# New order of work at the joints between the sites of a two-block float32 model

## Chip, core and metric

The kernel runs on one core of one Trainium2 chip. Its time is the device time of one execution in microseconds (us). Before the change three runs gave 1433.32, 1435.70 and 1436.69 us; the median is 1435.7.

## What is computed

256 tokens of width 1024 go through two blocks, all in float32. The first block has two layers (latent attention, convolution, Fourier and gating branches) and ends with a root-mean-square norm. The second block has six sites, in this order: feed-forward, mixer, feed-forward, feed-forward, mixer, feed-forward.

```python
def second_block(x, ...):
    for layer in range(2):
        g = norm_gains[layer]
        h = rmsnorm(x, g[0])
        x = x + 0.5 * rmsnorm(swiglu(h, w_gate[layer, 0], w_up[layer, 0], w_down[layer, 0]), g[1])
        h = rmsnorm(x, g[2])
        x = x + rmsnorm(token_mixer(h, ...), g[3])
        h = rmsnorm(x, g[4])
        x = x + 0.5 * rmsnorm(swiglu(h, w_gate[layer, 1], w_up[layer, 1], w_down[layer, 1]), g[5])
    return x
```

`swiglu(h)` is `(silu(h @ w_gate) * (h @ w_up)) @ w_down` with 2816 hidden features. Between the last sum of one site and the first product of the next lie two norms over all 1024 features: that of the site's result and that of the new `x`.

## The kernel before

**Layout.** `x` (the tile `residual`) holds two token tiles t = 0, 1 of 128 tokens, each in two half rows hf = 0, 1 of 512 features. Products take each number as a high and a low part (`HH`, `HL` for the input, `WH`, `WL` for weights), so one product is three matmuls: high by high, low by high, high by low. Weights come by DMA in slots of 1 MB through a ring of three (`weight_ring`). A slot holds two units of 128 x 1024. Of each unit ScalarE makes the high part (`high(U)`, L992) and VectorE the low part (`low(U)`, L1573). SyncE fills a ring slot again when the low part of the last unit of its old content is counted in `s_low`; `turn` gives each unit its place in that count. `WH` and `WL` hold six units.

**A site's start.** TensorE turns `x` into feature-major chunks c = 0..7 of 128 features (`site_norm`, transposes at L2447, with a few products of constants at L2438 between them). ScalarE copies each chunk with the norm's gain as `HH` (L1032), VectorE takes the rest as `HL` (L1608). The first two units (`first_units`) run chunk by chunk over the high parts (L2474, L2475), then over the low parts (L2479). The norm's own factor is not needed for these products: squares of `x` are summed on ScalarE (`x_square`, L996), VectorE and ScalarE make the inverse root (`inverse`), and TensorE spreads it over the partitions (`norm_sum`, L2464); ScalarE copies it to `norm_row` (L1041). What is read from the products afterwards is multiplied by `norm_row`.

**Feed-forward site.** Each pair of hidden chunks takes six units: gate, up, one earlier down unit, gate, up, down. At the end the last three down units a+4, a+5, a+6 are added into banks 4 to 7, which hold the result y(t, hf). The unit a+4 goes over both tiles; then each of y(0,0), y(0,1), y(1,0), y(1,1) gets a+5 and a+6 in turn.

**Mixer site.** Its products of queries, keys and values take 24 units. The first scores (L2608) need the first query block and its key block, which VectorE reads out by L1756 (`evicted`). VectorE's order there is: units 0 and 1 read out, `low` of units 4 and 5, unit 2 read out. The scores need units 0 and 2.

**A site's end.** ScalarE sums the squares of each y(t, hf) in that order (`site_tail`, L1051) and takes the root per tile (L1057). VectorE multiplies y by the gain (`gained`, L1634), takes the reciprocal (L1639) and adds each half row to `x` (`update`, L1644). Per tile it is: gained 0, gained 1, reciprocal, update 0, update 1. At the end of a feed-forward site ScalarE first makes the high parts of three units of the next site (`ahead`), then loads the table for the square root (L1120), then starts on the squares.

**Block joint.** The last product of the first block is scaled by VectorE (L1278). GpSimd adds three of the four half rows to `x` (L671) and VectorE one (L1282). ScalarE sums squares (L1008), VectorE scales `x` (`final_scaled`, L1582), tile by tile, with `low` of units 0, 2 and 1 of the first site between these steps. The first site starts with the units 0 and 1, one gate and one up.

Each engine works through its instructions in the order in which they are written; waits are on semaphores.

## Time and profile before

| | |
|---|---|
| median of three runs | 1435.7 us |
| the profiled execution | 1436.06 us |
| its span, first to last instruction | 1434.1 us |
| TensorE (PE) busy | 1398.1 us, 97% |
| VectorE (DVE) busy | 1018.7 us, 71% |
| ScalarE (ACT) busy | 726.7 us, 51% |
| GpSimd (POOL) busy | 86.7 us, 6% |
| DMA | 243.03 MB, mean 169 GB/s |
| mean granted TensorE clock | 0.997 of full speed |

TensorE is busy for nearly all of the span, but that includes the products of constants at the joints. The time between the last useful product of one site and the first of the next is what an order of work at a joint can change. Matmul durations overlap: of a row that holds several, the time to the start of the next row tells more than its length.

### The profile page before, as it was taken

How to read it: one execution, taken by the hardware profiler on the slowest of the kernel's cores; microseconds unless marked ns; L12 is line 12 of the kernel's file. 1: busy time of each engine (PE TensorE's matmuls, PEld its weight loads, DVE VectorE, ACT ScalarE, POOL GpSimd, SP SyncE). 2: the span in 40 equal slices, each digit the busy share in tenths (PEclk: the TensorE clock that was granted, in tenths of full speed). 3: DMA queues.
4: the chain of work that ended last, by engine and by line, in shares of the span. 5: the costliest groups of instructions: out<-in, count | busy, mean ns of one | idle time of the engine just before them, and what ended most of it. 6: DMA issues, size and time to landing. Idle time of an engine off the chain costs nothing.

```text
span 1434.1 us, 22170 instructions
## 1 busy us (share of the span) xinstructions
PE 1398.1 (97%) x8053; PEld 1159.8 (81%) x8053; DVE 1018.7 (71%) x1693; ACT 726.7 (51%) x1244; POOL 86.7 (6%) x103
## 2 busy tenths in 40 slices
PE   5999999999999999999999999999999999999998
PEld 2778747869768888888888888888888888888887
DVE  2588454469677777787686777877777876877776
ACT  3433264345565444475664444654445756644444
POOL 0301211220110000000200000000000002000000
PEclk9999999999999999999999999999999999999999
DMA  9622184275235655754345556646655643455662
GB/s 354 195 88 89 59 285 175 88 221 150 88 133 170 198 189 175 248 176 146 118 133 176 175 193 193 211 153 202 197 183 177 195 142 118 133 176 178 202 196 98
DMA packets 185654, 243.03 MB, mean 169 GB/s; under 512 B 4560, under 2 KB 154608, under 8 KB 185456
## 3 DMA queue, kind: packets, MB, share of 16 engines
q1 hardware_dynamic: 182272, 229.43, 49.9%
q0 software_dynamic: 2736, 10.55, 2.2%
q10 hardware_dynamic: 576, 2.10, 0.4%
q8 instruction: 46, 0.75, 0.2%
q14 instruction: 24, 0.20, 0.0%
HBM read 241.01 MB, written 1.05 MB: 169 GB/s over the span
## 4 chain that ended last, share of the span: by engine, by line
PE 69%; DVE 12%; DMA 9%; ACT 5%; issue 4%; POOL 0%; SPq 0%; DVEq 0%; ACTq 0%; POOLq 0%
PE bank L1977 33%; PE bank L2496 13%; PE bank L2498 7%; DMA weight_ring<-in_w_ffn_up 5%; DVE weights_low L1573 3%; ACT weights_high L992 3%; DVE arena L1567 2%; PE bank L2104 2%; DMA weight_ring<-in_w_ada 2%; DMA weight_ring<-in_w_ffn_down 2%; PE bank L1958 1%; DMA weight_ring<-in_w_in 1%; PE bank L2324 1%; PE bank L2474 1%; PE bank L2475 1%
## 5 line engine op out<-in xcount | busy, mean ns | idle before, releaser
L1573 DVE TENSOR_TENSOR weights_low<-weight_ring,weights_high 128x1024 fp32r<-128x1024 f32 x328 | 393.3, 1223 | 128.8 <-ACT weights_high L992 128.7
L992 ACT ACTIVATE weights_high<-weight_ring 128x1024 fp32r<-128x1024 f32 x328 | 334.6, 1048 | 102.1 <-PE bank L1977 62.0
L2496 PE MATMUL bank<-input_split,weights_high 128*128 128x512 f32 x1280 | 319.5, 391 | 0.0
L2496 PEld LDWEIGHTS bank<-input_split,weights_high 128*128 128x128 f32 x1280 | 234.7, 188 | 45.0
L2498 PEld LDWEIGHTS bank<-input_split,weights_low 128*128 128x128 f32 x1280 | 174.6, 190 | 12.5
L2498 PE MATMUL bank<-input_split,weights_low 128*128 128x256 f32 x1280 | 178.5, 282 | 0.0
L1977 PE MATMUL bank<-weights_high,hidden_high 128*128 128x512 f32 x352 | 138.8, 394 | 1.2 <-DVE hidden_low L1682 1.2
L1066 ACT ACTIVATE silu_gate<-gate_sum 128x256 f32<-128x256 f32 x88 | 36.7, 418 | 202.0 <-DVE gate_sum L1660 200.5
L1977 PE MATMUL bank<-weights_low,hidden_high 128*128 128x512 f32 x352 | 137.9, 392 | 0.0
L1977 PE MATMUL bank<-weights_high,hidden_low 128*128 128x512 f32 x352 | 137.0, 389 | 0.0
L1977 PE MATMUL bank<-input_split,weights_high 128*128 128x256 f32 x576 | 105.6, 285 | 0.0
L1072 ACT ACTIVATE hidden_high<-hidden 128x256 fp32r<-128x256 f32 x88 | 36.8, 418 | 129.8 <-DVE hidden L1673 123.7
L1977 PE MATMUL bank<-weights_high,input_split 128*128 128x256 f32 (+1 forms) x384 | 90.2, 323 | 0.5 <-issue 0.5
L1977 PEld LDWEIGHTS bank<-input_split,weights_high 128*128 128x128 f32 x576 | 89.5, 192 | 1.1 <-DVE qk_feature_major L1756 0.7
L1977 PE MATMUL bank<-hT_high,first_high 128*128 128x512 f32 (+1 forms) x248 | 89.6, 361 | 0.2 <-DVE weight_ring_low L1253 0.2
L1977 PE MATMUL bank<-hT_high,weight_ring_low 128*128 128x512 f32 (+1 forms) x248 | 86.9, 350 | 0.0
L1977 PE MATMUL bank<-input_split,weights_low 128*128 128x256 f32 x288 | 81.4, 283 | 0.0
L1977 PEld LDWEIGHTS bank<-weights_high,hidden_high 128*128 128x128 f32 x352 | 66.4, 189 | 14.3 <-issue 2.8
L1977 PEld LDWEIGHTS bank<-weights_high,hidden_low 128*128 128x128 f32 x352 | 66.1, 188 | 14.5
L1977 PEld LDWEIGHTS bank<-weights_low,hidden_high 128*128 128x128 f32 x352 | 66.4, 189 | 10.7
L1977 PEld LDWEIGHTS bank<-weights_high,input_split 128*128 128x128 f32 x384 | 64.4, 190 | 8.6 <-issue 3.5
L1682 DVE TENSOR_TENSOR hidden_low<-hidden,hidden_high 128x256 fp32r<-128x256 f32 x88 | 37.4, 425 | 43.7 <-ACT hidden_high L1072 43.7
(358 smaller groups left out, 2267.5 us busy)
## 6 DMA issues: line engine op xcount, KB each, us to landing
weight_ring<-in_w_ffn_gate SPq DMA_DIRECT2D x44, 1024.0 KB, 5.3
weight_ring<-in_w_ffn_up SPq DMA_DIRECT2D x44, 1024.0 KB, 5.3
weight_ring<-in_w_ffn_down SPq DMA_DIRECT2D x44, 1024.0 KB, 4.9
weight_ring<-in_w_in SPq DMA_DIRECT2D x32, 1024.0 KB, 5.3
weight_ring<-in_w_ada SPq DMA_DIRECT2D x24, 1024.0 KB, 6.0
weight_ring<-in_w_out SPq DMA_DIRECT2D x16, 1024.0 KB, 5.0
weight_ring<-in_w_in SPq DMA_DIRECT2D x24, 512.0 KB, 4.8
gain_row<-in_norm_gains POOLq DMA_DIRECT2D x6, 512.0 KB, 4.1
```

The lines of the kernel that those rows point to most:

```text
L992: A(unit_in(WH, U), unit_source(U), ACT.Copy).then_inc(s_high, 1)
L1066: A(sgate[:, par, :], gsum[:, par, :], ACT.Silu).then_inc(s_silu, 1)
L1072: A(HBH[:, par if to is None else to, :], hbuf[:, par, :], ACT.Copy).then_inc(s_hh, 1)
L1567: STT(accv, src, w, accv, ALU.mult, ALU.add).then_inc(*done("conv_tap", L, j, k))
L1573: TTn(unit_in(WL, U), unit_source(U), unit_in(WH, U).bitcast(F32), ALU.subtract).then_inc(s_low, 1)
L1682: TTn(HBL[:, to, :], hbuf[:, par, :], HBH[:, to, :].bitcast(F32), ALU.subtract).then_inc(s_hl, 1)
L1958: last = mm(b[32 * k:32 * k + 32, :], CS[:, 4 * q + k, :], quarters(n)[:, k, :], start=(q == 0), stop=(q == 1), skip_group_check=True)
L1977: last = mm(o, lhs(x), rhs(y), start=start and m == 0, stop=stop and m == 2, skip_group_check=True)
L2104: last = mm(b[out_rows, 0:ncol], lhs(k), hT[:, k, 0:ncol], start=(k == 0), stop=(k == KD - 1))
L2324: mm(b[:, 0:keys], Q[0:QK, h, seg * T + qt * P:seg * T + (qt + 1) * P], K[0:QK, h, k0:k0 + keys], start=True, stop=True).then_inc(*done("s ...
L2496: mm(b[:, :].rearrange("p (h n) -> p h n", h=2), unit_in(WH, U)[:, k, :], HX[:, k, :, :], start=(k == 0), stop=False, skip_group_check=True)
L2498: last = mm(b[:, 0:T], unit_in(WL, U)[:, k, :], HH[:, k, :], start=False, stop=(k == KD - 1), skip_group_check=True)
```

## The change

It rearranges the work at all six joints, and adds one instruction on GpSimd and two on VectorE per feed-forward end.

1. Block joint: the first site starts with units 0 and 2 (both gate units of the first slot). VectorE adds three of the four half rows itself; `final_scaled` is cut into five parts, of which (1, 0) comes in two quarters; the high parts of units 1 and 3 and their low parts come later, unit 3's after the load of the Silu table.
2. `x` is turned in two portions: chunks 0 to 3 of both tiles first, and chunks 4 to 7 after the products of chunk 2 (`rest_turned`). The second product of constants is half as wide.
3. At a site's end the half row (1, 0) is added in two quarters before (1, 1) is multiplied by the gain. After a feed-forward site the sum of squares of x(0, 1) moves from ScalarE to VectorE (`tensor_tensor_reduce` over 512 columns).
4. Feed-forward end: a+4 and a+5 are added to y(0,0) and y(0,1) together, then a+6; then each of y(1,0), y(1,1) gets all three. VectorE makes the low parts of a+5 and a+6 before the steps that they stood behind. ScalarE makes the high part of only two units of the next site before the squares; those of the third and fourth follow the roots of tile 0 and tile 1. The low part of the third is made by GpSimd, and VectorE counts it in `s_low` after the last `HL`.
5. Site start: the norm's spreading product comes two chunks later in a feed-forward site and one whole unit later in a mixer; `high` and `low` of the next units and the read-out of the up unit change places.

Renamed semaphores (`q_copied`) and arguments that only pass `rest_turned` on are left out here.

```diff
-X_BANK = (4, 5, 2, 3, 6, 7, 6, 7)
+X_BANK = ((4, 5, 1, 3, 6, 7, 6, 7),) + ((4, 5, 2, 3, 6, 7, 6, 7),) * 5
...
-ADDED = [{(0, 1), (1, 1)}, {(1, 1)}]
+ADDED = [{(0, 1), (1, 1)}, {(0, 1), (1, 0), (1, 1)}]
...
+                if i < 5 and kind == "ffn":
+                    third = unit_base[i + 1] + EARLY - 2
+                    pool.wait_ge(s_high, turn[third] + 1)
+                    pool.tensor_tensor(unit_in(WL, third), unit_source(third), unit_in(WH, third).bitcast(F32), ALU.subtract).then_inc(*done("third_low", i + 1))
...
-                    act.wait_ge(s_used, step(U - SPLIT + 1, j, 6))
+                    act.wait_ge(s_used, step(U - SPLIT + 1 + (U == SPLIT + 1), j, 6))
...
```

ScalarE:

```diff
-                        if t == 1:
-                            x_square(0, 0, 0)
-                            x_square(0, 0, 1)
                 act.wait_ge(*at("final_squares", t, 1))
                 A(stat[:, 8 + t:9 + t], stat[:, 2 * t + 1:2 * t + 2], ACT.Sqrt, bias=stat[:, 28 + t:29 + t], scale=1.0 / D).then_inc(*done("final_root", t))
-                if t == 0:
-                    high(1)
-            high(3)
+            high(1)
...
-                if i:
+                after_ffn = i and SITES[i - 1][0] == "ffn"
+                if i and not after_ffn:
                     x_square(i, 0, 0)
-                    x_square(i, 0, 1)
-                if i and SITES[i - 1][0] == "ffn":
-                    high(unit_base[i] + EARLY - 1)
                 for c in range(KD):
+                    if c == 4:
+                        x_square(i, 1 if i else 0, 0)
...
-                for hf in range(2):
-                    x_square(i, 1, hf)
+                    A(HH[:, c, :], B[X_BANK[i][c]][:, half * T:(half + 1) * T], ACT.Copy, scale=vT[:, 2, R_PRE + 8 * i + c:R_PRE + 8 * i + c + 1]).then_inc(*done("input_high", i, c))
+                if not after_ffn:
+                    x_square(i, 0, 1)
+                if i == 0:
+                    x_square(i, 1, 0)
+                x_square(i, 1, 1)
                 act.wait_ge(*at("x_mean", "ready", i))
                 A(stat[:, 8:10], stat[:, 6:8], ACT.Sqrt).then_inc(*done("rms_ready", "site", i))
-                high(unit_base[i] + 4)
                 if SITES[i][0] == "ffn":
                     A(stat[:, 60:61], eps[:, 0:1], ACT.Silu)
+                if i == 0:
+                    high(3)
+                if SITES[i][0] == "mix":
+                    high(unit_base[i] + 4)
                 act.wait_ge(*at("norm_sum", i))
                 A(norm_row, B[4][:, 0:T], ACT.Copy).then_inc(*done("norm_row", i))
-                high(unit_base[i] + 5)
+                if SITES[i][0] == "mix":
+                    high(unit_base[i] + 5)
 
             def site_tail(i):
                 for t in range(2):
...
+                            if t and i < 5 and SITES[i][0] == "ffn":
+                                x_square(i + 1, 0, 0)
...
+                    if i < 5 and SITES[i][0] == "ffn":
+                        high(unit_base[i + 1] + EARLY - 2 + t)
...
+                high(a + 4)
                 silu(0, f0 + 1, f0 if n else None)
-                if n:
-                    high(a + 6)
-                    hidden_high(0, f0 + 1, None)
-                else:
-                    hidden_high(0, f0 + 1, None)
-                    high(a + 6)
+                hidden_high(0, f0 + 1, None)
+                high(a + 5)
+                high(a + 6)
...
+                high(a + 6)
                 hidden_high(1, f + 2, None, to=2)
-                high(a + 6)
-                for U in ahead[1:]:
+                for U in ahead[1:2]:
...
```

VectorE, the block joint, the site's start and end:

```diff
+                    low(0)
+                    out_scaled(1, 0, 0)
+                    low(2)
+                    out_scaled(1, 0, 1)
+                    out_scaled(1, 1, 0)
+                    out_scaled(1, 1, 1)
+                    return
...
+            final_inverse(0)
+            final_scaled(0, slice(0, 512), 0)
+            final_inverse(1)
+            final_scaled(1, slice(0, 256), 0, "first")
+            final_scaled(1, slice(256, 512), 0)
+            final_scaled(0, slice(512, 1024), 1)
+            final_scaled(1, slice(512, 1024), 1)
...
+                if i and SITES[i - 1][0] == "ffn":
+                    dve.wait_ge(*at("third_low", i))
+                    CP(stat[:, 61:62], eps[:, 0:1]).then_inc(s_low, 1)
+                if i and SITES[i - 1][0] == "ffn":
                     low(unit_base[i] + EARLY - 1)
+                if i == 0:
+                    low(1)
...
+                        if (t, hf) == (0, 1) and i and SITES[i - 1][0] == "ffn":
+                            dve.wait_ge(*at("x_mean", "first tile", i))
...
+                gained(0, 0)
+                gained(0, 1)
+                scale(0)
+                update(0, 0, slice(0, 512))
+                update(0, 1, slice(512, 1024))
+                gained(1, 0)
+                if i == 5:
+                    gained(1, 1)
+                    scale(1)
+                    update(1, 0, slice(0, 512))
+                else:
+                    if SITES[i][0] == "ffn":
+                        dve.wait_ge(*at("x_new", i, 0, 1))
+                        dve.tensor_tensor_reduce(out=XN2[:, 0, 512:1024], in0=X[:, 0, 512:1024], in1=X[:, 0, 512:1024], scale=1.0, scalar=0.0, op0=ALU.mult, op1=ALU.add, accum_out=stat[:, 1:2]).then_inc(*done("x_mean", "first tile", i + 1))
+                    scale(1)
+                    update(1, 0, slice(0, 256), "first")
+                    update(1, 0, slice(256, 512))
+                    gained(1, 1)
+                update(1, 1, slice(512, 1024))
...
+                if n == 0:
+                    low(3)
                 gate_parts(0, a + 1)
-                up_parts(0, a + 2)
-                low(a + 4)
                 dve.wait_ge(*at("norm_row", i))
                 gate_scaled(0, f0 + 1)
+                up_parts(0, a + 2 if n else 3)
+                multiplied(0, f0 + 1)
+                low(a + 4)
+                hidden_low(0, f0 + 1)
                 low(a + 5)
-                multiplied(0, f0 + 1)
-                hidden_low(0, f0 + 1)
...
+                low(a + 5)
                 dve.wait_ge(s_used, a + 4)
                 dve.wait_ge(s_silu, f + 2)
                 TTn(hbuf[:, 1, :], B[3][:, 0:T], sgate[:, 1, :], ALU.mult).then_inc(s_h, 1)
-                low(a + 5)
+                low(a + 6)
                 hidden_low(1, f + 2, to=2)
-                low(a + 6)
-                for U in ahead[1:]:
+                for U in ahead[1:2]:
...
```

TensorE:

```diff
+                        part = (1, 0, "first") if t and c < 2 else (t, c // 4)
+                        pe.wait_ge(*(at("x_new", i - 1, *part) if i else at("final_scaled", *part)))
+                        last = tr(B[X_BANK[i][c]][:, half * T + t * P:half * T + (t + 1) * P], X[:, t, c * P:(c + 1) * P], ident)
...
-                warm(1)
-                turned(0, (4, 5, 6, 7))
-                turned(1, (0, 1, 2, 3, 4, 6, 5, 7))
+                warm(1, 256)
+                turned(1, (0, 1, 2, 3))
+                return lambda: (turned(0, (4, 6)), turned(1, (4, 6)), turned(0, (5, 7)), turned(1, (5, 7)))
...
+                step_to = 1 if i else 2
                 for q in range(2):
-                    pe.wait_ge(s_low, turn[U + q] + 1)
+                    pe.wait_ge(s_low, turn[U + step_to * q] + 1)
                 for c in range(KD):
...
+                    if c == 2:
+                        rest_turned()
...
-                    if site is not None and k == 3:
+                    if site is not None and k == 5:
...
+                second = 1 if n else 2
+                for r in hand_over(0) + hand_over(second):
...
+                first_units(i, a, (B[0], B[second]), T, rest_turned)
+                for r in hand_over(3 - second) + hand_over(3):
                     pe.wait_ge(*at(*r))
-                gate_up(1, a + 2, f0 if n else None, None, i)
+                if n:
+                    gate_up(1, a + 2, f0, None, i)
+                else:
+                    for U, b, site in ((1, 1, i), (3, 3, None)):
+                        pe.wait_ge(s_low, turn[U] + 1)
+                        wide_product(B[b], U, site).then_inc(s_used, 1)
...
+                lasts = ((1, a + 4, f), (0, a + 5, f + 1), (2, a + 6, f + 2))
+                for rest in (lasts[:2], lasts[2:]):
                     for hf in range(2):
-                        for par in range(2):
-                            pe.wait_ge(s_hl, f + 1 + par)
-                            pe.wait_ge(s_low, turn[a + 5 + par] + 1)
-                            last = down_row(2 * par, a + 5 + par, t, False, par == 1, (hf,))
-                            if t and hf:
-                                last.then_inc(s_used, 1)
-
-            def mix(i, n):
+                        for par, U, ready in rest:
+                            pe.wait_ge(s_hl, ready)
+                            pe.wait_ge(s_low, turn[U] + 1)
+                            down_row(par, U, 0, False, U == a + 6, (hf,))
+                for hf in range(2):
+                    for par, U, ready in lasts:
+                        last = down_row(par, U, 1, False, U == a + 6, (hf,))
+                        if hf:
+                            last.then_inc(s_used, 1)
...
+                products(2, 3)
                 norm_sum(i)
-                products(2, 4)
+                products(3, 4)
                 scores(0)
...
```

## Rows read from the trace of the kernel before

**Rows 1.** The page, groups of instructions: busy us, mean ns, idle before and releaser

```profile
L1573 DVE TENSOR_TENSOR weights_low<-weight_ring,weights_high 128x1024 fp32r<-128x1024 f32 x328 | 393.3, 1223 | 128.8 <-ACT weights_high L992 128.7
L992 ACT ACTIVATE weights_high<-weight_ring 128x1024 fp32r<-128x1024 f32 x328 | 334.6, 1048 | 102.1 <-PE bank L1977 62.0
```

**Rows 2.** Waits of TensorE: line, releaser: us in total, times, longest us

```profile
PE bank L2447 <- DVE residual L1644: 2.1, 4, 1.4
```

**Rows 3.** Timeline of TensorE, feed-forward to feed-forward: start us, us, instruction [idle before]

```profile
927.30 1.02 PE L2438 MATMUL bank<-const_base 128*128 128x512 f32 x2
...
930.27 1.32 PE L2447 MATMUL bank<-const_base,residual 128*128 128x128 f32 x8 [0.21 <-DVE residual L1644]
931.34 0.36 PE L2474 MATMUL bank<-input_split,weights_high 128*128 128x256 f32 x1
...
937.18 0.87 PE L2496 MATMUL bank<-input_split,weights_high 128*128 128x512 f32 x3
```

**Rows 4.** Timelines of ScalarE and of VectorE at the same joint

```profile
927.50 0.60 ACT L1051 ACTIVATE silu_gate<-bank 128x512 f32<-128x512 f32 x1 [0.28 <-PE bank L1977]
...
928.22 0.29 ACT L1057 ACTIVATE stat<-stat 128x1 f32<-128x1 f32 x1
...
930.63 2.30 ACT L1032 ACTIVATE input_split<-bank,vectors_T 128x256 fp32r<-128x256 f32 x6
...
929.46 1.41 DVE L1644 SCALAR_TENSOR_TENSOR residual<-x_scaled,stat,residual 128x512 f32<-128x512 f32 x2
931.14 2.45 DVE L1608 SCALAR_TENSOR_TENSOR input_split<-bank,vectors_T,input_split 128x256 fp32r<-128x256 f32 x6 [0.27 <-ACT input_split L1032]
```

**Rows 5.** Timelines of GpSimd and VectorE where both are at work

```profile
275.46 1.29 POOL L671 TENSOR_TENSOR residual_ctx<-residual_ctx,scaled_out 128x512 f32<-128x512 f32 x1 [2.27 <-DVE scaled_out L1278]
...
274.03 0.75 DVE L1221 TENSOR_SCALAR gated<-residual,stat 128x1024 f32<-128x1024 f32 x1
...
275.49 1.82 DVE L1221 TENSOR_SCALAR gated<-residual,stat 128x1024 f32<-128x1024 f32 x1
...
418.69 2.04 DVE L1582 SCALAR_TENSOR_TENSOR residual<-residual,stat,gain_row 128x512 f32<-128x512 f32 x2
```

**Rows 6.** Timelines of TensorE and VectorE, second feed-forward to mixer

```profile
1115.22 1.02 PE L2438 MATMUL bank<-const_base 128*128 128x512 f32 x2
...
1125.18 0.68 PE L2464 MATMUL bank<-scaled_out,const_base 128*128 128x128 f32 x4
...
1131.55 0.49 PE L2608 MATMUL bank<-qk_feature_major 64*128 64x128 f32 x4
...
1129.26 0.42 DVE L1756 SCALAR_TENSOR_TENSOR qk_feature_major<-bank,scaled_out 128x256 f32<-128x256 f32 x1
```

**Rows 7.** Timeline of TensorE, first feed-forward to mixer

```profile
611.28 1.02 PE L2438 MATMUL bank<-const_base 128*128 128x512 f32 x2
...
630.09 0.49 PE L2608 MATMUL bank<-qk_feature_major 64*128 64x128 f32 x4
```

**Rows 8.** Timeline of TensorE, mixer to feed-forward

```profile
739.17 1.02 PE L2438 MATMUL bank<-const_base 128*128 128x512 f32 x2
...
748.60 0.86 PE L2496 MATMUL bank<-input_split,weights_high 128*128 128x512 f32 x3
```

**Rows 9.** Timelines of TensorE and ScalarE, block joint to the first down unit

```profile
424.26 1.82 PE L2447 MATMUL bank<-const_base,residual 128*128 128x128 f32 x8 [2.07 <-DVE residual L1582]
425.74 0.56 PE L2474 MATMUL bank<-input_split,weights_high 128*128 128x256 f32 x1
...
432.50 0.86 PE L2496 MATMUL bank<-input_split,weights_high 128*128 128x512 f32 x3
...
438.55 0.40 PE L1977 MATMUL bank<-weights_high,hidden_high 128*128 128x512 f32 x1
...
431.61 1.28 ACT L1039 ACT_TABLE_LOAD   x1
```

**Rows 10.** A stretch of the block joint: us, busy of each engine, PEclk, DMA share, GB/s

```profile
425.70:428.00 2.30, 2.30 (x13) 2.30 (x12) 1.88 (x5) 1.67 (x6) 0.04 (x1) 0.53 1.09 386
```

87 lines of the change are left out of this document (32 added, 55 removed).

## Prediction

> **What bounds the kernel now.** Read the busy shares first, in the table above: TensorE is busy for 97% of the span, VectorE for 71%. What the others do is hidden as long as it is ready in time: each weight unit costs ScalarE 1.05 us and VectorE 1.22 us [rows 1], beside some 2.8 us of products. Then read TensorE's waits: at the joints after the sites it stands only 2.1 us in all for VectorE's new `x`, the longest time 1.4 us [rows 2]. So little of a joint is idle; most of it is filled by products of constants. Its true price is the time from the last useful product (call it E, the start of the row of L2438) to the end of the first two units. The timeline shows it: E is 927.30, the transposes of tile 1 start at 930.27, the first product at 931.34, the next unit at 937.18 [rows 3]. That is 2.97, 4.04 and 9.88 us after E. Of these, 5.84 us are the 48 products of the first two units and 1.07 us eight transposes.
>
> I forecast each joint in this way: when is the first piece of x(1,0) there, when does the first product start, and what follows it. Everything is told for one joint and carried over.
>
> **1. The piece of x that comes last.** ScalarE starts the squares of y(1,1) at E+0.20 and the root at E+0.92; it ends at E+1.21 [rows 4]. From the root to VectorE's addition lie the reciprocal and two hand-overs, about 0.3 us. Before, VectorE was still busy with `gained` then, and added the half row from E+2.16 on (929.46). It took 1.41/2 and a hand-over of 0.1: E+2.97. In the new order the addition may start at E+1.50, and a quarter (256 columns) is half as long, so about 0.42 us and 0.1: transposes at E+2.02. From the first transpose to ScalarE's copy are 0.36 us (930.27 to 930.63), from there to where the next engine sees it 0.51 (931.14) [rows 4]. So the first product is at E+2.89 instead of E+4.04. But only half of the transposes are behind it: eight more, 1.07 us, now stand among the products. The first two units then end at 2.89 + 5.84 + 1.07 = E+9.80, against 9.88. So cutting the half row gains 0.08 us where VectorE is free. The gain in latency is nearly all given back, because the transposes used to run while TensorE would wait anyway.
>
> **2. GpSimd's new subtraction.** It is the term of which I am least sure and which decides the sign. After a feed-forward site ScalarE makes the third unit's high part behind the root of tile 0. The new order of the last down units completes y(0,0) and y(0,1) after 15 and 18 of 36 products of 512 columns (48 of 256 columns take 5.84 us [rows 3], so 0.12 each and about 0.23 for 512), so at E-4.8 and E-4.1, and ScalarE reaches that high part at about E-2.6 and ends at E-1.6. GpSimd then subtracts 128x1024 of two SBUF tensors. The trace has no such instruction; the nearest is 1.29 us for 512 columns [rows 5], so I take 2 x 1.29 = 2.58 us. When VectorE and GpSimd both need SBUF the trace shows that one stands still: the same 128x1024 scaling takes VectorE 0.75 us alone and 1.82 us when it is issued 0.03 us after GpSimd's start, and it ends 0.55 us after GpSimd does (277.31 and 276.75) [rows 5]. Two additions with two SBUF inputs take 2.04 us beside GpSimd and 1.41 without [rows 4, 5]. VectorE is busy with the two updates of tile 0 until E-0.7. Then comes `gained(1,0)`, which reads PSUM and in which GpSimd gets in. It holds SBUF from E-0.7 to E+1.9, and the new sum of squares (two SBUF inputs, about 0.7 us), which stands ahead of the reciprocal and the quarter, waits for it: it ends at E+2.6, the quarter is seen at E+3.3, the first product at E+4.2, the first two units end at E+11.1. That is 1.3 us later than in step 1. Bounds: nothing, if GpSimd runs before or after; 2 us, if it starts before the second update and holds that up as well.
>
> The Trainium skill (SBUF — State Buffer, section "SBUF: two separate sides") says that the pair of ports is an exclusive lock, for VectorE with two SBUF inputs too, and that whoever starts first has it for the whole instruction. The trace agrees for the scaling (1.82 for 0.75); for the two additions it shows only 0.63 us lost. By the rule the loss is the 1.3 us above; by a sharing as in the additions it would be 0.6.
>
> **3. Feed-forward to feed-forward** (one joint): 9.88 becomes 11.1, **1.2 us lost**. What follows holds: the hidden part must be ready for the first down unit 6.0 us after the first two units, and the chain of the later `norm_sum` (1.2 instead of 0.7 us in), copy, gate product, Silu, product, `low(a+4)` 1.22, hidden low part takes about 5.7. The slot of gate weights is asked for 10 us later, because the third unit's count now comes after the last `HL`; its next unit is needed only after 8.8 us of other products, which covers the load.
>
> **4. Feed-forward to mixer** (two joints). Here `norm_sum` goes behind the third unit, and the scores come one unit after it instead of two. VectorE's order is not changed: from `norm_sum` (1125.18) to the read-out of unit 2 (1129.26 and 0.42, 0.07 to hand over) are 4.6 us [rows 6], since two `low` stand in between. TensorE needs it after its own 0.44 and one unit of 2.95, so after 3.4: **a new wait of about 1.2 us**. Now the sums up to the first scores. Before, at the second such joint: 1131.55 - 1115.22 = 16.33 us [rows 6]. After: 11.1 + 2.95 + 4.6 = 18.6, **2.3 us lost**. Before, at the first: 630.09 - 611.28 = 18.81 us [rows 7]; there the load of `alibi` holds up the third unit's weights, ScalarE reaches the squares later, and TensorE waits for them. The new order takes the third unit out of that queue. After: the same 18.6, **0.2 us gained**.
>
> **5. Mixer to feed-forward** (two joints). No GpSimd work here. Before, TensorE was never idle between 739.17 and 748.60 [rows 8]: 9.43 us. After it is 9.80 by step 1, since the shorter product of constants leaves gaps for the quarters: 0.37 us each, **0.7 us lost**.
>
> **6. Block joint.** Before, tile 1's transposes start at 424.26 after 2.07 us of idling, and the first product at 425.74 [rows 9]. Ahead of x(1,0) go away: `low` of unit 1 (1.2), the second half of tile 0 with its hold-up by GpSimd (half of 2.04 and the 0.6 above, about 1.3 [rows 5]), half its own length (0.3); VectorE's two more additions cost about 0.3 net, as GpSimd's 1.29 each had to be waited for. So 2.5 us earlier: 421.75. The first product is 0.87 behind that instead of 1.48: 422.6. The eight transposes of the second portion come back (1.07). The clock: the granted clock in 425.70 to 428.00 was 0.53, near the lower level of 1.2 GHz, right after the idling of 2.07 us [rows 9, 10]; the first two units took 432.50 - 425.74 = 6.76 instead of 5.84. With about 1.2 us of idling I expect 2.4 GHz, as in all other joints. They end at 422.6 + 5.84 + 1.07 = 429.5, 3.0 us earlier than 432.50. Of this the head of the site gives some back: unit 3's high part (1.05) now stands behind three sums of squares, the root and the Silu table (1.28 [rows 9]), its low part (1.22) behind that, and the gate's sums behind both. I take 0.4 us of waiting for unit 3 and 0.7 for the hidden part, so the first down unit starts 1.9 us before the old 438.55: **1.9 us gained**. Bounds: 3.0 if nothing waits, 0.7 if table and high part lie wholly on the path.
>
> **7. The end.** Behind the last product the order is the same squares, root, `gained(1,1)`, two additions and store. Nothing.
>
> **Sum:** 1.9 + 0.2 - 1.2 - 2.3 - 0.7 = -2.1, so 2.1 us slower. The profiled execution took 1436.06 us (span 1434.1 and 2.0 around it): 1438.2. The median lies 0.4 below it: **1437.8 us**, 0.15% above 1435.7. What this kernel's measurement can tell from no change is 0.2%, 2.9 us.
>
> **Rivals.**
> - *GpSimd does not hold up VectorE.* The subtraction falls where VectorE reads PSUM or idles, or is shared. For it: only one VectorE instruction with two SBUF inputs lies in that stretch. Against: the scaling of rows 5. Three joints get 1.3 back: 3.9 - 2.1 = 1.8 us gained, 1433.9.
> - *Neither does the mixer wait, and the block joint gives all.* If the read-out is not late, 2 x 1.2 more, and 1.1 from step 6: 5.3 gained, 1430.4. Against: the 4.6 us stand in the trace and VectorE's order there is untouched.
> - *The other side: the clock falls at the joints.* In step 2 TensorE idles from E+1.7 (product of constants, four transposes, half a product) to E+3.3, 1.6 us. Waits of 1.4 us kept the full clock, 2.07 us lost it [rows 2, 9, 10]. If 1.6 us loses it, each of three joints pays 0.9 for the products and 0.4 for the transposes (1.48 for 1.07): 3.9 more, 6.0 lost, 1441.7. It decides from between 1.4 and 2.07 us of idling.
> - *The block joint gains nothing*, since unit 3 is late by table and high part, and the refill of its slot, asked for 3 us later, holds up the next pair: 1.9 less, 1439.7.
>
> The Trainium skill (GPSIMD Engine Reference, section "Key points") also names VectorE instructions with two SBUF inputs as those that contend with GpSimd; that speaks for step 2 against the first rival.
>
> **Chances.** Forecast, with a loss of 0.5 to 4 us: 0.47 (of it 0.30 within 0.2%, 0.17 slower). First rival 0.20 (0.15 within, 0.05 faster). Second 0.15, faster. Clock 0.11 and block joint 0.07, of it 0.17 slower and 0.01 within. Faster 0.20, same 0.46, slower 0.34. The range takes in the first rival and the fourth and the near parts of the second and third: 1432.0 to 1441.2; the forecast's own is 1436.2 to 1439.7.
>
> **What would show it.** Step 1: first transposes of tile 1 at E+2.0 and first product at E+2.9 after a mixer. Step 2: after a feed-forward site, GpSimd's row of about 2.5 us, the reduction on VectorE ending with or after it, transposes past E+3. Step 4: a wait of L2608 for L1756 of about 1.2 us, twice. Step 6: clock 1.00 behind the block joint, first product near 422.6, a wait for unit 3's low part. Transposes at E+2 behind feed-forward sites would make the forecast wrong towards faster; a PEclk under 0.9 there, towards slower.

## The result: 1.0% slower, outside the forecast's range

The new kernel takes **1449.0 us** (median of 4 runs, 1444.5 to 1451.4) against 1434.6 us for the kernel before on the same chip (4 runs, 1433.3 to 1436.7): a ratio of 1.0095, 95% interval 1.0073 to 1.0117. The forecast was 1437.8 us, its range ended at 1441.2. The direction had a chance of 0.34 and the size had none.

The profiled execution is the slowest of the four: 1451.39 us, span 1449.6, so 15.5 us more than the 1434.1 of before. The page's first line, busy times of the engines:

```profile
PE 1401.5 (97%) x8053; PEld 1162.9 (80%) x8053; DVE 1027.0 (71%) x1707; ACT 726.0 (50%) x1238; POOL 90.7 (6%) x104
```

TensorE's busy time is up by only 3.4 us; the rest is idle time. TensorE's waits show where (line, releaser: us in total, times, longest):

```profile
PE bank L2016 <- DVE hidden_low L1719: 7.5, 5, 2.9
PE bank L2660 <- DVE qk_feature_major L1795: 4.9, 6, 1.5
PE bank L2487 <- DVE residual L1666: 4.3, 3, 1.4
...
PE bank L2487 <- DVE residual L1589: 0.6, 1, 0.6
```

(A row says: the instruction of TensorE at that line of the kernel waited for the engine, tile and line behind the arrow.) The third line is the answer to [rows 2]: the joints' own waits grew from 2.1 to 4.3 us. But the largest group is one that the prediction never priced: the down products of the feed-forward sites waiting for `hidden_low`, 7.5 us in five places, one of 2.85 us.

**The joints came out nearly as forecast.** Timeline of TensorE in the new kernel, first the block joint (E is 417.39 now, 417.00 before), then feed-forward to feed-forward (E is 932.44):

```profile
421.64 0.74 PE L2487 MATMUL bank<-const_base,residual 128*128 128x128 f32 x4
422.57 0.36 PE L2515 MATMUL bank<-input_split,weights_high 128*128 128x256 f32 x1 [0.19 <-ACT input_split L1031]
...
429.29 1.32 PE L2539 MATMUL bank<-input_split,weights_high 128*128 128x512 f32 x5
...
433.12 2.14 PE L2539 MATMUL bank<-input_split,weights_high 128*128 128x512 f32 x8 [0.41 <-DVE weights_low L1581]
...
436.97 0.47 PE L2016 MATMUL bank<-weights_high,hidden_high 128*128 128x512 f32 x1 [0.78 <-DVE hidden_low L1719]
...
932.44 1.02 PE L2477 MATMUL bank<-const_base 128*128 128x512 f32 x2
...
935.77 0.83 PE L2487 MATMUL bank<-const_base,residual 128*128 128x128 f32 x4 [1.44 <-DVE residual L1666]
936.75 0.36 PE L2515 MATMUL bank<-input_split,weights_high 128*128 128x256 f32 x1 [0.15 <-ACT input_split L1031]
...
943.49 1.32 PE L2539 MATMUL bank<-input_split,weights_high 128*128 128x512 f32 x5
```

Block joint [rows 9]: a wait of 0.41 for unit 3 (forecast 0.4) and 0.78 for the hidden part (0.7), first down unit at 436.97, which is E+19.58 instead of E+21.55 (forecast E+19.65). The marks on the way look exact as times of the span (first product 422.57 for 422.6, first two units done at 429.29 for 429.5), but E itself came 0.39 later in this execution: told from E they are E+5.18 for 5.6 and E+11.90 for 12.5. Feed-forward to feed-forward [rows 3]: first product at E+4.31 (4.2), first units done at E+11.05 (11.1).

Of the 1.97 us at the block joint most is the clock. The run before_chain (section 6) has the block joint of the kernel before, with the same idling of 2.07 us (E is 416.64), and its clock stayed up. A stretch and a row of its TensorE:

```profile
426.00:428.00 2.00, 2.00 (x19) 2.00 (x18) 1.51 (x5) 1.37 (x5) 0.00 (x0) 1.00 1.11 390
...
436.84 0.40 PE L1977 MATMUL bank<-weights_high,hidden_high 128*128 128x512 f32 x1
```

There the first down unit starts at E+20.20 in the old order. So 1.35 of the 1.97 are the fall of the clock that the profiled execution of before had and this one had not, and 0.62 are the new order.

**Where the time went.** From one E to the next each site has a length. Split at the first down unit (in a mixer, the first scores), the profiled executions differ by this much, new minus before, in us:

| stretch | block joint, site 1 | mixer 1 | ffn 2 | ffn 3 | mixer 2 | last ffn | sum |
|---|---|---|---|---|---|---|---|
| joint, forecast | -1.9 | -0.2 | +0.4 | +1.2 | +2.3 | +0.4 | +2.1 |
| joint, measured | -1.97 | -0.41 | +0.26 | +1.17 | +3.62 | +0.27 | +2.94 |
| rest of the site, measured | +5.38 | +1.23 | +0.26 | +3.51 | +0.64 | +1.10 | +12.12 |

("ffn" is a feed-forward site. The 0.4 us that are left of the 15.5 lie ahead of the first E.) The forecast's row is nearly the measured one, but for mixer 2, where 1.6 us are a fall of the clock. The last row was forecast as zero.

What happened inside the sites is one row each. Timeline of TensorE, then stretches of the same kernel (us, busy of PE, PEld, DVE, ACT, POOL, PEclk, DMA share, GB/s):

```profile
465.23 0.79 PE L2016 MATMUL bank<-weights_high,hidden_high 128*128 128x512 f32 x1 [2.85 <-DVE hidden_low L1719]
...
785.49 0.49 PE L2016 MATMUL bank<-weights_high,hidden_high 128*128 128x512 f32 x1 [0.88 <-DVE hidden_low L1719]
...
976.47 0.70 PE L2016 MATMUL bank<-weights_high,hidden_high 128*128 128x512 f32 x1 [1.86 <-DVE hidden_low L1719]
...
1296.70 0.49 PE L2016 MATMUL bank<-weights_high,hidden_high 128*128 128x512 f32 x1 [1.14 <-DVE hidden_low L1719]
```

```profile
465.00:467.00 2.00, 1.77 (x4) 1.49 (x5) 1.48 (x3) 1.53 (x2) 0.00 (x0) 0.50 0.95 328
467.00:469.00 2.00, 2.00 (x6) 1.52 (x5) 1.97 (x4) 0.00 (x0) 0.00 (x0) 0.50 0.78 238
...
976.00:978.00 2.00, 1.53 (x4) 1.24 (x5) 1.47 (x2) 1.78 (x2) 0.00 (x0) 0.65 0.95 302
978.00:980.00 2.00, 2.00 (x7) 1.52 (x6) 1.97 (x4) 0.00 (x0) 0.00 (x0) 0.50 0.81 241
...
1131.00:1133.00 2.00, 2.00 (x12) 2.00 (x11) 0.69 (x3) 0.47 (x1) 0.00 (x0) 0.50 0.68 246
```

The waits stand in a feed-forward site's second round (its second pair of hidden chunks, the next six units), at the second chunk of the pair, called the second slot. Before, the same places showed 0.56, 0.41, none and 0.26 us. And PEclk reads 0.50, the lower level (1.2 instead of 2.4 GHz), in some 6.8 us behind the first wait and 3.4 behind the third, and again behind the joint at 1125. Over slices of 2 us, the time times what PEclk lacks to 1 adds up to 3.4 + 1.7 + 1.7 = 6.8 us lost to the clock. Before it was 1.7 from the first E on, all in the block joint [rows 10], and another 1.7 at 32 us, in the first block. The four runs point the same way: mean granted clock 0.995, 0.995, 0.997 and 0.999 with 1451.4, 1450.0, 1448.1 and 1444.5 us. The clock is not the whole loss, though: the run at 0.999 is still 9.9 us above the median of before.

### The profile page after: what moved, and what is told of

Same layout as the page of the kernel before. It is cut to its first block, busy times and chain, and to the rows that moved or that the text cites. A ratio compares the mean times of both kernels' runs of the same rounds, so it can differ in the third digit from the quotient of the medians.

```text
span 1449.6 us, 22166 instructions
## 1 busy us (share of the span) xinstructions
PE 1401.5 (97%) x8053; PEld 1162.9 (80%) x8053; DVE 1027.0 (71%) x1707; ACT 726.0 (50%) x1238; POOL 90.7 (6%) x104
## 4 chain that ended last, share of the span: by engine, by line
PE 77%; DVE 11%; DMA 4%; ACT 4%; issue 3%; SPq 0%; POOL 0%; DVEq 0%; ACTq 0%; POOLq 0%
PE bank L2016 36%; PE bank L2539 17%; PE bank L2541 9%; DMA weight_ring<-in_w_ffn_up 2%; DVE weights_low L1581 2%; DVE arena L1575 2%; PE bank L2143 2%; ACT weights_high L996 2%; DMA weight_ring<-in_w_ada 1%; PE bank L1997 1%; DVE residual L1666 1%; PE bank L2363 1%; PE bank L2515 1%; PE bank L2388 1%; PE bank L2516 1%
## 5 line engine op out<-in xcount | busy, mean ns | idle before, releaser
L1581 DVE TENSOR_TENSOR weights_low<-weight_ring,weights_high 128x1024 fp32r<-128x1024 f32 x325 | 389.3, 1222 | 130.6 <-ACT weights_high L996 130.6
L2541 PEld LDWEIGHTS bank<-input_split,weights_low 128*128 128x128 f32 x1280 | 174.6, 190 | 12.5
```

Source lines behind the costliest of these rows:

```text
L1581: TTn(unit_in(WL, U), unit_source(U), unit_in(WH, U).bitcast(F32), ALU.subtract).then_inc(s_low, 1)
L2541: last = mm(b[:, 0:T], unit_in(WL, U)[:, k, :], HH[:, k, :], start=False, stop=(k == KD - 1), skip_group_check=True)
```

## Experiments

**The theories.** "Refill" is SyncE's request for new weights in a ring slot, "the wait for `hidden_low`" is TensorE's wait at a down unit for the low part of the hidden features. A: the losses inside the sites come from refills that are asked for late, and from VectorE's idling in the sites' heads while it waits for the row of norms. Its rivals: the loads are covered, as the prediction had it, and the loss lies at the joints, above all in GpSimd's hold on SBUF. B (after the first four runs): when the slots' refills are asked for decides alone. C (after the next four): a chain of loads sets the pace of the first two rounds.

"ratio" is against runs of the kernel before on the same chip, "1st" to "last" are the lengths of the six sites in the profiled execution, from E to E.

| kernel | us | ratio, 95% | 1st | mix | ffn | ffn | mix | last |
|---|---|---|---|---|---|---|---|---|
| before | 1434.6 | 1 | 194.3 | 127.9 | 188.1 | 187.9 | 125.4 | 188.1 |
| new | 1449.0 | 1.0095 (1.0073 to 1.0117) | 197.7 | 128.7 | 188.7 | 192.6 | 129.7 | 189.4 |
| heads | 1449.1 | 1.0096 (1.0079 to 1.0112) | 197.0 | 128.7 | 188.7 | 193.2 | 128.1 | 189.7 |
| counts | 1447.1 | 1.0084 (1.0064 to 1.0104) | 194.6 | 130.3 | 189.3 | 190.0 | 129.8 | 189.1 |
| third_dve | 1444.1 | 1.0064 (1.0047 to 1.0081) | 194.6 | 127.4 | 189.2 | 192.3 | 126.8 | 189.3 |
| block_only | 1436.0 | 1.0007 (0.9997 to 1.0017) | 195.2 | 127.6 | 187.8 | 188.0 | 125.5 | 188.2 |
| fourth | 1443.8 | 1.0082 (1.0065 to 1.0099) | 194.5 | 128.7 | 188.9 | 190.7 | 128.1 | 189.2 |
| joined | 1439.3 | 1.0040 (1.0026 to 1.0054) | 194.7 | 127.6 | 188.9 | 188.6 | 127.0 | 189.2 |
| joined_norm | 1436.4 | 1.0025 (1.0015 to 1.0034) | 192.6 | 126.3 | 189.0 | 188.7 | 125.8 | 188.9 |
| joined_down | 1439.6 | 1.0042 (1.0028 to 1.0056) | 194.6 | 127.5 | 189.1 | 188.4 | 127.0 | 189.3 |
| chain | 1432.8 | 0.9987 (0.9975 to 0.9999) | 193.1 | 126.3 | 189.0 | 187.8 | 125.9 | 188.5 |
| after_chain | 1442.3 | 1.0056 (1.0042 to 1.0070) | 193.8 | 130.3 | 188.3 | 189.8 | 129.7 | 188.4 |
| before_chain | 1431.9 | 0.9978 (0.9969 to 0.9987) | 192.1 | 127.6 | 187.4 | 188.0 | 125.4 | 187.5 |
| block_chain | 1431.1 | 0.9980 (0.9971 to 0.9989) | 192.2 | 128.8 | 187.4 | 187.9 | 125.4 | 187.5 |
| block_mix_chain | 1430.1 | 0.9966 (0.9954 to 0.9978) | 192.1 | 126.2 | 187.4 | 187.8 | 125.5 | 187.5 |
| block_mix_down | 1430.4 | 0.9971 (0.9961 to 0.9982) | 192.3 | 126.3 | 187.7 | 187.9 | 125.5 | 187.5 |

The kernel before ran in every batch: its medians were 1434.8 us beside heads, counts, third_dve and block_only, 1432.6 beside fourth and the three called joined, 1434.4 beside chain, before_chain, block_chain and block_mix_chain, 1434.1 beside after_chain and block_mix_down. The ratios are those on record; they differ from the quotients of the medians by up to 0.0007. Medians of different batches are compared below only with that in mind. In the edits shown, `...` stands for what is left out, and lines that begin with # say where they stand; that of section 4 is a summary and not lines of the kernel.

### 1. Who holds up VectorE: third_dve

```
-pool.tensor_tensor(unit_in(WL, third), ...).then_inc(*done("third_low", i + 1))
 # VectorE, behind the eight HL:
-dve.wait_ge(*at("third_low", i)); CP(...).then_inc(s_low, 1)
+low(unit_base[i] + EARLY - 2)
```

> The new kernel, with the third unit's low part subtracted by VectorE behind the site's eight low parts of the input instead of by GpSimd. Theory A: behind the feed-forward sites VectorE's two additions of tile 0 take 1.42 us again instead of 3.55, and the first product comes at E+3.0 instead of E+4.3 at three joints; the first two units end about 1.2 us earlier. But the refills are asked for no earlier, so in the feed-forward to feed-forward site the wait for hidden_low grows by as much (1.9 to 3.0 us) and the clock falls for longer: of 3 x 1.2 us only 1.5 to 2.5 come out, 1447. Rival (SBUF contention is the main loss of the change): 3 x 1.3 and more come out, 1445 or less.

Measured 1444.1: 5 us faster than the new kernel, which is the rival's figure and not theory A's (the intervals of the two ratios just overlap). But 9.3 us above the kernel before are left, so it isn't the main loss. VectorE and GpSimd in the new kernel at E = 932.44, then VectorE in this one at E = 927.45:

```profile
930.36 3.55 DVE L1666 SCALAR_TENSOR_TENSOR residual<-x_scaled,stat,residual 128x512 f32<-128x512 f32 x2
933.83 0.68 DVE L1657 TENSOR_TENSOR x_scaled<-bank,gain_row 128x512 f32<-128x512 f32 x1
934.43 0.67 DVE L1681 CUSTOM_DVE_ANT_0 x_scaled<-residual 128x512 f32<-128x512 f32 x1
...
935.04 0.15 DVE L1661 RECIPROCAL stat<-stat 128x1 f32<-128x1 f32 x1
...
930.89 2.47 POOL L695 TENSOR_TENSOR weights_low<-weight_ring,weights_high 128x1024 fp32r<-128x1024 f32 x1 [183.28 <-ACT weights_high L996]
```

```profile
925.37 1.42 DVE L1701 SCALAR_TENSOR_TENSOR residual<-x_scaled,stat,residual 128x512 f32<-128x512 f32 x2
926.70 0.69 DVE L1692 TENSOR_TENSOR x_scaled<-bank,gain_row 128x512 f32<-128x512 f32 x1
927.30 0.68 DVE L1724 CUSTOM_DVE_ANT_0 x_scaled<-residual 128x512 f32<-128x512 f32 x1
...
928.69 0.16 DVE L1696 RECIPROCAL stat<-stat 128x1 f32<-128x1 f32 x1 [0.70 <-ACT stat L1086]
```

The two additions of tile 0 take 3.55 us beside GpSimd's 2.47 and 1.42 without. GpSimd starts 0.53 us after the first addition. If that one takes its usual 0.71 (half of 1.42), the second stands until GpSimd is done (933.36); the row ends at 933.91, 0.55 later, just as in [rows 5]. The Trainium skill (SBUF — State Buffer, section "SBUF: two separate sides") calls the shared ports an exclusive lock for the whole instruction: the trace agrees, 2.13 us lost for 2.47. So the hold-up of step 2 is real, at three joints: first products come at E+2.97 here instead of E+4.31. It costs 1.34 and not 2.13, since VectorE, left alone, stands 0.70 for ScalarE's root ahead of the second reciprocal. That is 3 x 1.34 = 4.0 us; TensorE stands no longer than 0.15 us at these joints now, and in this execution the clock fell at none of them. The third feed-forward site paid with a longer wait (2.35 instead of 1.86) and a fall of the clock, as theory A had it.

### 2. When the slots are refilled: counts and fourth

```
 # counts: VectorE, right behind the sum of squares of the first tile
+dve.wait_ge(*at("third_low", i + 1)); CP(...).then_inc(s_low, 1)
 # first site's gate slot:
-sp.wait_ge(s_low, last_unit[n - RING] + 1)
+sp.wait_ge(s_low, 2)
```

> The new kernel, with the third unit counted earlier: behind a feed-forward site VectorE counts GpSimd's subtraction right behind the sum of squares (about E+2.6 instead of E+8.9), so the refill of that gate slot is asked for about 6 us earlier, and the refill of the up slot, asked for at E+10.2, no longer shares the queue with it. In the block joint the gate slot's refill waits for units 0 and 2 alone. Theory A: in the feed-forward to feed-forward site the up unit lands 2 us earlier, the wait of 1.86 us for hidden_low shrinks to 0.8 or less and the clock stays full: that site is 2.5 to 3 us shorter (188.65 and 192.60 are the two sites' lengths now; it is the second). In the first site little (0.3 us), since there the up slot comes last. 1446. Rival (the loads are covered by 8.8 us of other products, as the prediction had it): nothing moves, 1449.

Refills around the third feed-forward site's joint, before (E = 927.30), new (E = 932.44), and here (E = 930.15):

```profile
924.74 0.38 SPq L564 DMA_DIRECT2D weight_ring<-in_w_ffn_gate  x1
935.83 0.38 SPq L564 DMA_DIRECT2D weight_ring<-in_w_ffn_up  x1
```

```profile
941.67 0.38 SPq L564 DMA_DIRECT2D weight_ring<-in_w_ffn_gate  x1
942.64 0.38 SPq L564 DMA_DIRECT2D weight_ring<-in_w_ffn_up  x1
```

```profile
933.09 0.38 SPq L578 DMA_DIRECT2D weight_ring<-in_w_ffn_gate  x1
940.35 0.38 SPq L578 DMA_DIRECT2D weight_ring<-in_w_ffn_up  x1
```

Before, the gate slot was asked for at E-2.56, 11 us ahead of the up slot. In the new kernel it is asked for at E+9.23, 1 us ahead of it, and both loads are under way together: ScalarE then waits for the up weights until E+17.65, where before it got them at E+13.86 (ScalarE before, then in the new kernel):

```profile
941.16 1.06 ACT L992 ACTIVATE weights_high<-weight_ring 128x1024 fp32r<-128x1024 f32 x1 [0.69 <-DMA weight_ring<-in_w_ffn_up]
```

```profile
950.09 2.01 ACT L996 ACTIVATE weights_high<-weight_ring 128x1024 fp32r<-128x1024 f32 x2 [1.23 <-DMA weight_ring<-in_w_ffn_up]
```

In this run the wait for `hidden_low` fell from 1.86 to 0.79 us, no slice at the lower clock followed, and the site took 190.0 instead of 192.6. Theory A's 2.5 to 3 us is what was measured (2.6: 1.1 of waiting, the rest the clock that did not fall); the prediction's "which covers the load" is refuted. In the first site the wait stayed (2.94), as said, and behind the first mixer it grew from 0.88 to 1.45. The median moved by 1.9 only, inside the intervals; here the clock fell behind two other joints.

```
 # fourth: ScalarE, first site
+high(3)                                    # ahead of the root
 A(stat[:, 8:10], ..., ACT.Sqrt); A(..., ACT.Silu)
-high(3)
```

> The new kernel, with ScalarE making the fourth unit's high part in the first site ahead of the root and the Silu table instead of behind them; nothing else. Theory B (what decides inside a site is when the slots' refills are asked for: here the up slot, 2.6 us later than before because low(3) stands behind the table): low(3) ends about 1.4 us earlier, the up refill is asked for at E+14.2 instead of E+15.7, TensorE's waits for unit 3 (0.41) and for the first hidden part (0.78) go, and its wait of 2.9 us in the second slot shrinks to about 1.5; the first site takes 192 us instead of the 194.6 that it takes at the full clock. About 1446.5 in all. Rival (the second slot is late by the order of VectorE's and ScalarE's other work): the early waits go but the later one grows by as much, the site stays at 194.6.

The first down unit came at E+18.30 instead of E+19.58 (both early waits gone), the up refill at E+14.07 instead of E+15.70. But the second slot's wait only shrank from 2.9 to 2.44, and the profiled site took 194.5, with 1.7 us at the lower clock behind that wait. The ratio is 1.9 us better, inside the intervals. Both theories were too simple: the wait shrank by about the difference between what the hidden part gained (1.8 in the first round) and what TensorE gained (1.28).

### 3. Is it the order of VectorE's head? heads

```
 # VectorE, later feed-forward sites: old order
 gate_parts(0, a + 1)
+up_parts(0, a + 2); low(a + 4)
 dve.wait_ge(*at("norm_row", i)); gate_scaled(0, f0 + 1)
```

> The new kernel, with the heads of the three later feed-forward sites (2, 3 and 5) in the old order again: low(a+4) and the second reduction stand ahead of VectorE's wait for the row of norms, ScalarE makes high(a+4) ahead of it. Theory A (VectorE idles 1.2 to 1.5 us for that row and hands the idling on to the second slot's hidden part; after a feed-forward site the load of the third slot is what comes last): the two sites behind a mixer lose the waits of 0.88 and 1.14 us for hidden_low almost wholly (0.4 and 0.2 left), about 1.3 us in all; the site behind a feed-forward site keeps its wait of 1.86 us and its stretch at the lower clock. About 1447.5 us. Rival (the order of the head doesn't matter, all these waits come from the loads): nothing moves, 1449.

No gain: 1449.1. The two waits behind mixers did not go: 0.88 became 0.79, the one of 1.14 became 1.66, and the third feed-forward site got a wait of 2.44 us for its first hidden part in place of the later one of 1.86. So VectorE's idling of 1.2 to 1.5 us for the row of norms, which is plain in the trace, is not what costs: theory A fell in this point.

### 4. The block joint alone: block_only

```
 # against the kernel before: X_BANK of site 0, final_scaled in three pieces, head of site 0; else old
+new = i == 0        # transposes, squares, first_units
-new = True          # updates, third_low, lasts, norm_sum of all other joints
```

> The kernel before with the new order at the block joint alone (both gate units first, VectorE's three additions in order of arrival, head of the first site); all other joints old. Theory A: the block joint itself gains 1.6 to 2.0 us up to the first down unit, as in the new kernel, and the second slot of the same site loses 2.3 us of waiting and 3.1 us of lower clock again, because low(3) stands behind the Silu table and the up slot's refill is asked for 2.6 us later: the first site is 3.4 us longer than before, the others as before. 1438. Rival (the loss inside the first site comes from the new order at its tail and from GpSimd, thus from the next joint): 1.6 to 2.0 us faster than before, 1433.

```profile
435.46 0.47 PE L2073 MATMUL bank<-weights_high,hidden_high 128*128 128x512 f32 x1 [0.80 <-DVE hidden_low L1764]
...
464.02 0.49 PE L2073 MATMUL bank<-weights_high,hidden_high 128*128 128x512 f32 x1 [3.00 <-DVE hidden_low L1764]
```

Measured: neither faster nor slower (1.0007, -0.0003 to +0.0017). The first down unit starts at E+19.58 here too, 1.97 earlier than in before, and in the second round TensorE waits 3.00 us instead of 0.56: 2.44 given back. The site is 0.9 us longer than before, in an execution without a slice at the lower clock. So the loss inside the first site belongs to the block joint itself, and not to its tail or to GpSimd.

### 5. Together, and the mixers: joined, joined_norm, joined_down

```
 # joined: fourth's edit, the gate slot's wait for 2, and on VectorE
 update(0, 1, slice(512, 1024))
+low(unit_base[i + 1] + EARLY - 2)
 gained(1, 0)
-dve.tensor_tensor_reduce(...)     # first tile's second sum of squares
 scale(1); update(1, 0, ...); gained(1, 1); update(1, 1, slice(512, 1024))
+dve.tensor_tensor_reduce(...)
```

> The new kernel with the three mends together: fourth unit's high part first in the first site and its gate slot's refill freed by units 0 and 2; behind feed-forward sites VectorE subtracts the third unit between tile 0's additions and gained(1,0), where it idles, so GpSimd has nothing to do, and the first tile's second sum of squares goes behind the last addition. Theory B: first products at E+3.0 at all five joints, gate refill at about E+0.6 at the feed-forward to feed-forward joint, no wait over 1.5 us there; the sites take 192, 127.2, 189, 189, 126.7 and 189.3 us. 1437. Rival (the loss stays in the second slots by VectorE's order, whoever frees the slots): 1441.

Here VectorE subtracts the third unit between tile 0's additions and `gained(1,0)`, where it idles. Measured 1.0040: of the new kernel's 0.95% more than half is gone. First products at E+2.97 at all five joints, gate refill at E+0.66, 0.60 us of wait in the third feed-forward site; but 2.61 in the first.

```
 # joined_norm: mixers
-products(2, 3); norm_sum(i); products(3, 4)
+norm_sum(i); products(2, 4)
```

> As the run before (the three mends together), and in the mixers the sum over features stands ahead of the third and fourth unit again, as in the old order, so the first scores come two units behind it. If the wait of 0.99 us at the first scores and of 1.0 to 1.5 at the second ones is the price of the one unit's shift (step 4 of the prediction): both mixers 0.8 to 1.6 us shorter, 1435. If VectorE's read-outs are late whatever stands there: no change against the run before.

First the two late scores of the first mixer in joined, then all that is left of them in joined_norm:

```profile
629.20 0.49 PE L2743 MATMUL bank<-qk_feature_major 64*128 64x128 f32 x4 [0.99 <-DVE qk_feature_major L1862]
...
638.26 0.49 PE L2743 MATMUL bank<-qk_feature_major 64*128 64x128 f32 x4 [1.54 <-DVE qk_feature_major L1862]
```

```profile
619.73 0.68 PE L2576 MATMUL bank<-scaled_out,const_base 128*128 128x128 f32 x4 [0.74 <-DVE scaled_out L1685]
...
633.96 0.49 PE L2743 MATMUL bank<-qk_feature_major 64*128 64x128 f32 x4 [0.34 <-DVE qk_feature_major L1862]
```

Both mixers are 1.2 us shorter, the median 2.9. Of the two waits in each mixer step 4 had forecast only the first; the second (1.54 and 0.97 us, eight to nine us behind it) had not been forecast at all.

```
 # joined_down: heads of the feed-forward sites
+low(a + 7)
 gate_sum(1, a + 3, f0 + 2)
-low(a + 7)
```

> As the run of the three mends together, and VectorE makes the low part of the second down unit (a+7) ahead of the second slot's gate sums instead of behind them, so that the down slot is refilled 1.1 us earlier in every feed-forward site. From the traces the up unit of the second round lands about 13 us behind the down slot's refill and TensorE's wait in the second slot ends 9 us behind that. Theory B: the waits for hidden_low in the second slot, 1.3 us in the sites behind a mixer, shrink by about 1 us in four sites: 3 us less in all, 1434. Rival (the round is bound by the loads' rate or by the gate sums that now come 1.1 us later): no gain or a loss of 1 to 3 us.

No gain (1439.6 against 1439.3): asking for the down weights 1.1 us earlier (E+22.76 for 23.86, first site) lands them earlier, but the gate refill behind them is asked for at E+27.69, as without it (27.73).

### 6. The chain of loads: before_chain, chain, after_chain

The times at which VectorE starts `hidden_low` for the second chunk of a pair (slot 1), told from E of the first site, gave theory C. Before it is 26.2 in the first round and 46.6 in the second; in the new kernel 27.2 and 47.3; in joined_norm 25.3 and 45.1: 20 us apart each time, whatever TensorE does. Between the two lie the parts of a+8 and a+9, the gate and the up refill that they free, some 8 us of loading, and 9 us of work on what has landed. TensorE arrives 25 us behind its first down unit. So the joint's gain counts only if that chain starts earlier too.

```
-hidden_high(1, f0 + 2, None); high(a + 8)      # ScalarE
+high(a + 8); hidden_high(1, f0 + 2, None)
-hidden_low(1, f0 + 2); low(a + 8)              # VectorE
+low(a + 8); hidden_low(1, f0 + 2)
```

> The new kernel with one thing moved: unit a+8's high and low part ahead of the second slot's hidden part, in the four feed-forward sites. Theory C: the gate refill of the second round is asked for 1.5 us and the up refill 1.1 us earlier; the waits in the second slots (2.85, 0.88, 1.86 and 1.14 us) shrink by 0.5 to 0.8 each, and the clock falls behind them more seldom: 3 to 5 us faster than the new kernel, 1445. Rival (the waits come from the joints and the loads' rate alone): within 1 us of it, 1449.

```profile
461.70 0.49 PE L2090 MATMUL bank<-weights_high,hidden_high 128*128 128x512 f32 x1 [1.59 <-DVE hidden_low L1775]
...
780.45 0.49 PE L2090 MATMUL bank<-weights_high,hidden_high 128*128 128x512 f32 x1 [0.52 <-DVE hidden_low L1775]
...
970.24 0.49 PE L2090 MATMUL bank<-weights_high,hidden_high 128*128 128x512 f32 x1 [0.67 <-DVE hidden_low L1775]
...
1288.14 0.49 PE L2090 MATMUL bank<-weights_high,hidden_high 128*128 128x512 f32 x1 [0.46 <-DVE hidden_low L1775]
```

This is the sharpest of the tests: one move of one unit in the unmended new kernel, 1442.3, so 1.0095 becomes 1.0056. The waits fell from 2.85, 0.88, 1.86, 1.14 to 1.59, 0.52, 0.67, 0.46 (3.5 us together), and no slice at the lower clock follows any of them. The gate refill of the second round was asked for at E+27.96 instead of E+29.57, the up refill at E+29.30 instead of E+30.53. And the 20 us themselves shrank. VectorE's two `hidden_low` of the first site, in the new kernel and in after_chain, then in before and in before_chain:

```profile
444.58 0.42 DVE L1719 TENSOR_TENSOR hidden_low<-hidden,hidden_high 128x256 fp32r<-128x256 f32 x1 [0.48 <-ACT hidden_high L1082]
464.67 0.43 DVE L1719 TENSOR_TENSOR hidden_low<-hidden,hidden_high 128x256 fp32r<-128x256 f32 x1 [0.48 <-ACT hidden_high L1082]
...
442.69 0.42 DVE L1775 TENSOR_TENSOR hidden_low<-hidden,hidden_high 128x256 fp32r<-128x256 f32 x1
461.14 0.43 DVE L1775 TENSOR_TENSOR hidden_low<-hidden,hidden_high 128x256 fp32r<-128x256 f32 x1 [0.48 <-ACT hidden_high L1105]
```

```profile
443.22 0.43 DVE L1682 TENSOR_TENSOR hidden_low<-hidden,hidden_high 128x256 fp32r<-128x256 f32 x1 [0.48 <-ACT hidden_high L1072]
463.64 0.42 DVE L1682 TENSOR_TENSOR hidden_low<-hidden,hidden_high 128x256 fp32r<-128x256 f32 x1 [0.48 <-ACT hidden_high L1072]
...
442.53 0.42 DVE L1682 TENSOR_TENSOR hidden_low<-hidden,hidden_high 128x256 fp32r<-128x256 f32 x1
461.04 0.42 DVE L1682 TENSOR_TENSOR hidden_low<-hidden,hidden_high 128x256 fp32r<-128x256 f32 x1 [0.48 <-ACT hidden_high L1072]
```

20.09 became 18.45 and 20.42 became 18.51: one round is 1.6 to 1.9 us shorter for one unit moved.

> The kernel before, with one thing moved in the heads of its feed-forward sites: the high and the low part of unit a+8 are made ahead of the second slot's hidden part instead of behind it. Theory C (inside a site the pace of the first two rounds is set by a chain: hidden_low of the second slot, the parts of a+8 and a+9 behind it, the gate and the up refill that they free, 8 us of loading, and 9 us of work on what has landed; it takes 20.2 us from the one hidden_low to the next of its slot, whatever TensorE does): the refills are asked for 1.2 to 1.7 us earlier, and the waits of 0.56 and 0.41 us for hidden_low go. In the kernel before that is worth no more than these, about 1 us: same. Rival (TensorE waits for the first hidden_low then, which is 0.7 us later): 0.5 to 1 us slower in each of four sites.

Faster by 0.22% (0.9969 to 0.9987), some 3 us, more than the expected 1: the waits of 0.56, 0.41 and 0.26 are gone, and the second and the last feed-forward site are 0.7 and 0.5 shorter. The first is 2.2 shorter, of which 1.35 are the clock that stayed up in the block joint. Is it the clock, then, and not the move? Not alone: at the same mean granted clock the runs still differ, by 2.2 us at 0.999 (1431.4, two runs, against 1433.6, eleven runs) and by 2.8 at 0.998 (1432.7, three, against 1435.4, thirteen).

> The three mends and the mixer's old order of norm_sum, and unit a+8 ahead of the second slot's hidden part. Theory C: the waits in the second slots (2.2, 1.2, 0.7 and 1.0 us) shrink by 1.0 to 1.2 us each: first site 191.5 us instead of 192.6, the others 0.7 to 1 shorter; 3.5 us less than the run without it, so about even with the kernel before. Rival (the loads' rate is the bound, they only queue longer): no change, 0.25% slower than before.

0.9987, so 5.4 us less than joined_norm by the ratios, where 3.5 were expected. The waits are 1.46, 1.06, under 0.3 and 0.51: they shrank by 0.2 to 0.7 and not by 1.0 to 1.2. In the second feed-forward site the gate refill came 1.5 us earlier, but the three loads of that round then took 12.6 us until the up weights had landed, so there the loads' own time is part of the bound. The profiled executions of the two differ by 1.1 us only (joined_norm's was the fastest of its ten), so where the rest of the 5.4 comes from is open.

### 7. Versions that beat both

```
 # block_chain: block_only + fourth + gate slot's wait for 2 + a+8 ahead
 # block_mix_chain: the first mixer's joint as in joined_norm too
-NEW_JOINTS = (0,)
+NEW_JOINTS = (0, 1)
 # block_mix_down: joined_down's edit on top
```

> The kernel before with the new order at the block joint alone, there with its mends (fourth unit's high part first, gate slot freed by units 0 and 2), and unit a+8 ahead in the four sites. Theory C: the block joint gains 3.2 us up to the first down unit, and 1.2 of it is lost again in the second slot; the first site takes 191.5 us instead of 194.3, and nothing else changes: 2 to 3 us faster than before. Rival (whatever the joint gains is given back to the chain of loads): within 0.5 us of before.

> As block_chain, and the first mixer's joint too in the new order (with VectorE subtracting the third unit while it idles, and the sum over features at its old place). In the run of the mends that mixer took 126.3 us against 127.9 before. If that holds alone: 1.6 us more than block_chain, 4 us faster than before. If it came from the new tail of the first site or from chance: no difference to block_chain.

> As block_mix_chain, and the down unit a+7's low part ahead of the second slot's gate sums, so that all three refills of the second round are asked for 1 to 1.5 us earlier. If the up unit's landing hangs on when the first of the three loads is asked for (they take 11.7 to 13.4 us together, 3 MB): the first site's wait of 1.68 us shrinks by about 1 us, 1429.3. If it hangs on the up refill's own time, or on VectorE's gate sums, which come 1.2 us later: no gain, 1430 to 1431.

block_chain is faster than before by 0.20%, but no better than before_chain alone. Its first site shows what the joint brings: the first down unit comes 1.9 us earlier than in before_chain (E+18.28 for 20.20), yet the site takes 192.2, the same as before_chain's 192.1, since 1.43 us are waited for again. block_mix_chain, with the first mixer's joint in the new order as well, has the lowest median: 1430.1 us, 0.9966 (0.9954 to 0.9978; the intervals overlap). Its mixer took 126.2 us against before_chain's 127.6. Asking for the down weights earlier as well (block_mix_down) brought nothing.

## Why the prediction was wrong, step by step

- **Step 1 held.** Behind a mixer the first product comes at E+2.97 (forecast 2.89) and the first units end at E+9.69 and 9.70 (9.80).
- **Step 2 held in size, not in place, and that is partly luck.** GpSimd took 2.47 us (2.58), from E-1.55 to E+0.92 instead of E-0.7 to E+1.9. It held up the second addition of tile 0, which the text had named as the upper bound's case, and not the sum of squares. GpSimd was done 1.0 us earlier than the step had it, but the rest of that addition and `gained(1,0)` then still stood ahead of the sum of squares, another 1.1 us; so this ended at E+2.60 for E+2.6 all the same. First product E+4.31 for 4.2.
- **Step 3 held for the joint (11.05 for 11.1) and failed in what follows it.** "Its next unit is needed only after 8.8 us of other products, which covers the load" looked at the gate slot alone. The refill came 11.8 us later relative to E, together with the up slot's, and it was the up weights that came late, at E+17.65 for 13.86 (asking for the gate slot earlier, in counts, took 2.6 us off that site).
- **Step 4 held for the first scores:** forecast 18.6; measured 18.40 and 19.95, the latter with 1.6 us of it lost to the lower clock. The wait is 0.99 us for 1.2. The second scores' wait, 0.95 to 1.53 us in each mixer, was missing from the sum.
- **Step 5 held** (0.26 and 0.27 lost for 0.37).
- **Step 6 is where the sum broke.** Up to the first down unit it came out (1.97 for 1.9), with two errors that cancel: the first units ended 3.6 us earlier relative to E and not 3.0 (what it calls about 1.3 is half of 1.41 and 0.63, not half of 2.04 and 0.6), and from there to the down unit it took 7.68 us instead of 7.15. The clock stayed at 1.00, as said; that is 1.35 of the 1.97, which the step had counted (6.76 for 5.84, 1.48 for 1.07) and which is gained only against an execution of before in which it falls. But "1.9 us gained" was carried to the end of the site, as if TensorE were the bound from there on. By TensorE's 97% that seems so; yet in the kernel before the wait at 464.19 (0.56) shows that the chain of loads already came last, though TensorE was 1.35 us late from the lower clock. Its slack was zero, and `low(3)` behind the Silu table put it 1 us later (`hidden_low` at E+27.2 for 26.2; in fourth, with unit 3's high part ahead of the table, 25.4). Instead of 1.9 gained, the first site is 3.4 longer: 2.3 more of waiting and 3.1 that go with the lower clock (3.4 by the slices), less the 1.97 gained. The fourth rival (0.07) had this mechanism, the refill that is asked for later, and priced it at no more than the joint's gain; at full clock (block_only: 2.44 given back for 1.97 gained) that price was nearly right for this site, and the other sites had no such term.
- **The clock.** The third rival put the fall at the joints' 1.6 us of idling. It fell there in some executions only (idle for 1.44 to 1.50 us at three joints in each of five profiled kernels: 5 of 15 fell, [rows 2] with 1.38 had not); more often it fell behind waits for `hidden_low` over 1.8 us, which the forecast did not contain (8 of 12 in all profiled kernels). Each fall cost 1.7 us, one 3.4.
- **Step 7 held.**

So 2.1 us of loss were forecast, 2.9 came where they were forecast, and 12.1 more inside the sites: 5.5 us of waits for `hidden_low` (6.73 less 1.23), 5.1 at the lower clock (3.4 + 1.7) and 1.8 at the mixers' second scores (12.4, for 12.1). after_chain takes away 3.5 of the 5.5 and every fall behind such a wait (5.1 us), joined_norm the third. (That is one execution of each. In after_chain's the clock fell behind two joints' 1.44 us instead, 3.4 us in all; its median of 1442.3 is 6.7 us under the new kernel's.) What is not settled is what decides in one execution whether the clock falls behind a given wait.

## What to carry to other kernels

A joint is not over when the engine is busy again. Follow each resource that the joint delays (a buffer's refill above all) to the next place where it is needed, two rounds on if need be, and look whether the trace of before has even a small wait there: a wait of 0.4 us was the sign here of a chain with no slack, and what the bound engine gained ahead of it came back as waiting (2.44 us for 1.97 in block_only), with interest where the clock fell. Moving one unit's conversions ahead on that chain was worth 0.22%; the reordered block joint alone was worth nothing, and on top of the move nothing that could be told.

## What the hardware showed that was not expected

- Whether TensorE's clock falls behind an idle stretch is not a matter of its length alone: 2.07 us ahead of the block joint lost it before [rows 10] and kept it in before_chain; 3.00 us kept it in block_only, 1.86 lost it in the new kernel.
- A 1 MB weight load asked for alone was used 5.3 us later (the up slot at E+8.53, its weights at E+13.86, third feed-forward site of before); asked for 1 us behind another it took 7.5 (E+10.20 to E+17.65 in the new kernel). Here the refill that lost its head start made its neighbour late, and not itself.
- All falls of the clock in the new kernel's and its variants' profiled executions but one cost the same 1.7 us by the slices, behind 1.44 us of idling as behind 3.32.
